# RWKV head-pair scan on one Trainium2 core: another order of the per-round work on TensorE, VectorE and ScalarE

## What is computed

```python
def update(s, w_t, k_t, v_t, kk_t, a_t):
    sa = einsum('ebhvk,ebhk->ebhv', s, kk_t)
    return s * w_t[..., None, :] - sa[..., :, None] * (kk_t * a_t)[..., None, :] \
           + v_t[..., :, None] * k_t[..., None, :]
# per token: s = update(s, ...); y = einsum('ebhvk,ebhk->ebhv', s, r)
# w, a: low-rank products of the input; kk: normalised keys
# out: ((group_norm(y) * ln_w + ln_b + bonus) * g) @ w_o
# bonus = (sum over a head of r * k_dir * r_k) * v;  g = sigmoid(x @ g1) @ g2
```

## Time and profile before

| | |
|---|---|
| median of 3 runs | 2686.97 us |
| the profiled execution | 2688.55 us, span 2686.8 us |
| busy in the span | PE 87%, PE weight loads 72%, DVE 35%, ACT 25%, POOL 32% |
| mean granted TensorE clock | 0.929 |
| first w16 of the scan to the last z | 1636.08 to 2201.91 us |

### The profile page before, as it was taken

How to read it: one execution, slowest core, us unless ns; L and a number is a source line. 1 busy time by engine, 2 the same in 40 slices (tenths; PEclk the granted TensorE clock), 3 DMA queues, 4 the chain that set the end, 5 groups by cost and what they waited for, 6 DMA issues and landing times. The chain is left out here.

```text
span 2686.8 us, 50294 instructions
## 1 busy us (share of the span) xinstructions
PE 2336.4 (87%) x22240; PEld 1946.8 (72%) x22240; DVE 944.5 (35%) x1475; ACT 662.8 (25%) x1032; POOL 854.6 (32%) x699
## 2 busy tenths in 40 slices
PE   5999877989699999999499957888888868999997
PEld 3778754555499999999169946777677755788786
DVE  3100175980500000222782035656565641200123
ACT  4110165421400000121321123433343312211111
POOL 2233200001144444343054413222332305466562
PEclk8999988989799999999599968999999978999998
DMA  5555600001021212111123421111111112232231
GB/s 215 215 204 210 221 33 16 1 32 47 17 70 62 62 62 62 63 63 48 18 85 111 134 59 33 39 36 37 39 39 37 22 64 63 78 94 94 86 97 68
DMA packets 139266, 204.06 MB, mean 76 GB/s; under 512 B 87783, under 2 KB 97511, under 8 KB 131912
## 3 DMA queue, kind: packets, MB, share of 16 engines
q1 hardware_dynamic: 139080, 201.26, 23.8%
HBM read 183.93 MB, written 17.30 MB: 75 GB/s over the span
## 5 line engine op out<-in xcount | busy, mean ns | idle before, releaser
L258 POOL CAST TMP_r<-WR 128x1024 fp32r<-128x1024 f32 x120 | 126.1, 1051 | 751.3 <-DMA WR<-in_ffn_w_dram 438.0
L277 PE MATMUL PS<-H_r,TMP_r 128*128 128x384 f32 (+1 forms) x1088 | 330.2, 359 | 15.4 <-DVE Y_r L492 15.4
L277 PE MATMUL PS<-Y_r,TMP_r 128*128 128x384 f32 (+1 forms) x1088 | 329.8, 358 | 3.7 <-DVE H_r L492 3.7
L260 POOL TENSOR_TENSOR WR_r<-WR,TMP_r 128x1024 fp32r<-128x1024 f32 x120 | 289.1, 2409 | 9.6
L415 DVE TENSOR_TENSOR P<-TMP,PS 128x768 f32 (+1 forms) x44 | 36.1, 821 | 562.4 <-PE PS L277 562.4
L277 PEld LDWEIGHTS PS<-H_r,TMP_r 128*128 128x128 f32 x1088 | 202.0, 190 | 33.0 <-DVE Y_r L492 17.3
L277 PEld LDWEIGHTS PS<-Y_r,TMP_r 128*128 128x128 f32 x1088 | 201.3, 189 | 19.3 <-DVE H_r L492 4.0
L277 PE MATMUL PS<-H_r,WR_r 128*128 128x384 f32 x736 | 191.6, 342 | 0.0
L268 POOL CAST TMP_r<-WR 128x1024 fp32r<-128x1024 f32 x68 | 84.3, 1240 | 322.0 <-DMA WR<-in_rw_w_rkv_dram 167.2
L270 POOL TENSOR_TENSOR WR_r<-WR,TMP_r 128x1024 fp32r<-128x1024 f32 x68 | 165.8, 2439 | 5.5
L398 ACT ACTIVATE TMP<-PS 128x768 f32<-128x768 f32 (+1 forms) x44 | 31.0, 705 | 525.9 <-PE PS L277 525.9
(11 more groups left out here) (307 smaller groups left out, 4480.5 us busy)
## 6 DMA issues: line engine op xcount, KB each, us to landing
WR<-in_ffn_w_dram SPq DMA_DIRECT2D x88, 512.0 KB, 3.5
TMP<-in_mod_w_dram SPq DMA_DIRECT2D x40, 1024.0 KB, 4.9
WR<-in_down_dram SPq DMA_DIRECT2D x44, 512.0 KB, 3.5
WR<-in_mix_w_in_dram SPq DMA_DIRECT2D x24, 512.0 KB, 7.0
WR<-in_rw_w_rkv_dram SPq DMA_DIRECT2D x24, 512.0 KB, 4.2
P<-in_mod_w_dram SPq DMA_DIRECT2D x4, 2048.0 KB, 21.7
vkr_dram<-extra SPq DMA_DIRECT2D x16, 384.0 KB, 4.8
scan_front<-vkr_dram SPq DMA_DIRECT2D x16, 384.0 KB, 3.1
```

Of the source, the lines that this page charges most:

```text
L258: nc.gpsimd.tensor_copy(hi, raw).then_inc(weights_hi, 1)
L260: nc.gpsimd.tensor_tensor(lo, raw, hi.bitcast(F32), ALU.subtract).then_inc(weights_split, 1)
L277: last = nc.tensor.matmul(PS[:, bank + b, 0:h1 - h0], w, x[:, h0:h1], start=k + p == 0, stop=k == CT - 1 and p == 2)
```

## The change

The same instructions are issued with the same operands, but in another order within a round, and two rounds' border is crossed by one of them:

- `lora(c, 0)` and its two Tanh evictions are issued at the end of the round for pair c (on PE between `kr` and `var`), instead of `lora(n, 0)` at the start of the next.
- PE: `oo_0` before A_0, `y32_1` before both; `cg` moves from between `mr_1` and `mr_2` to between `n_0` and `yt`, and DVE's `bonus` product behind `n_0`; kT_0, kT_1 and tV move in front of the chain.
- Between the chain's steps stand first the four transposes tB and tK, then KD_0, CK_0, KD_1, CK_1 and `kk`; before, it was the four products first, and then the transposes. BV_0 stands before `ys`, BV_1 between `ys` and `mean`.
- DVE: the mask of w16_0 stands before the first cumulative sum `scan_0` (L2583); `accr` comes after step 2 instead of step 4; the masks of KD and CK after steps 6 to 9 instead of 2 to 6.
- ACT: the evictions follow; `kc` and `ksq` of pair c now stand before tK_0 and tK_1 of pair n.
- SP and POOL keep their order.

The core of the diff (the tables `PEM`, `DV`, `AC`, `FRONT` repeat the loops' order):

```diff
                 if here(n):
-                    lora(n, 0)
...
                     transition(i, 0)
                     transition(i, 1)
+                if here(n):
+                    turned(n, 0)
+                if here(i):
+                    transition_rest(i)
+                    states(i, 0)
                     b = front("cg", i)
...
-                    transition_rest(i)
-                    states(i, 0)
                     pe.wait_ge(dve_done, DV["mL_1", i])
                     outputs_inside(i)
+                if here(n):
+                    turned(n, 1)
+                if here(i):
                     states(i, 1)
+                if here(n):
+                    pe.wait_ge(v_in, 16 * n + 16)
+                    tokens(n, "tV", VD[n % 2])
+                if here(i):
                     pe.wait_ge(dve_done, DV["n_1", i])
                     chain(i, 1)
...
                 if here(i):
-                    pe.wait_ge(act_done, AC["sq", i])
-                    PEM.done(turned_sums(3, FIN, 4), "var", i)
+                    outputs_carried(i)
+                if here(n):
+                    value_gram(n, 1)
+                if here(i):
+                    pe.wait_ge(act_done, AC["ys", i])
+                    PEM.done(nc.tensor.matmul(PS[:, 3, 0:L], HONES, YS, start=True, stop=True), "mean", i)
...
                     PEM.done(last, "kr", c)
-                if here(n):
-                    value_gram(n, 1)
-                if here(i):
+                    lora(c, 0)
+                if here(i):
+                    pe.wait_ge(act_done, AC["sq", i])
+                    PEM.done(turned_sums(3, FIN, 4), "var", i)
...
             for i, n, c in ROUNDS:
+                if here(i):
+                    level(i, 0, 0)
                 if here(n):
                     sums(n, 0)
                 if here(i):
-                    level(i, 0, 0)
                     level(i, 0, 1)
```

More of the change, by code:

```diff
@@ L1953, in hybrid_dit_kernel @@
         PEM = Marks(pe_done, (
[7 rows of a table removed]
-        DV = Marks(dve_done, (
[6 rows of a table removed]
-            (2, "kmax krec"), (0, "rec"), (2, "kmul"), (0, "f1 f2 z")))
[7 rows of a table added]
+        DV = Marks(dve_done, (
[6 rows of a table added]
+            (2, "kmax krec"), (0, "cen"), (2, "kmul"), (0, "rec f1 f2 z")))
         AC = Marks(act_done, (
[3 rows of a table removed]
[3 rows of a table added]
         PO = Marks(pool_done, ((1, "s00 s10 s01 s11 zero sub turn"),))
-        FRONT = ("l00 l10 l01 l11 A_0 A_1 cg KD_0 CK_0 KD_1 CK_1 tV tB_0 tK_0 tB_1 tK_1 kT_0 kT_1 kk BV_0 kr BV_1").split()
+        FRONT = ("l00 l10 l01 l11 A_0 A_1 cg kT_0 kT_1 tV tB_0 tB_1 tK_0 tK_1 KD_0 CK_0 KD_1 CK_1 kk BV_0 BV_1 kr").split()
         FRONT_TURN = {at: k for k, at in enumerate([at for at in PEM if at[0] in FRONT])}
@@ L2337, in scan_pe @@
                 if here(i):
[L2338 to L2343, removed]
+                    pe.wait_ge(dve_done, DV["y32_1", i])
+                    solve(i, "oo_1", [(1, j) for j in range(4)])
                 if here(n):
@@ L2387, in scan_pe @@
                 if here(i):
-                    chain(i, 6)
+                    pe.wait_ge(dve_done, DV["n_1", i])
+                    chain(i, 1)
                 if here(n):
@@ L2391, in scan_pe @@
                 if here(i):
+                    chain(i, 2)
+                if here(n):
+                    tokens(n, "tB_1", AA[1])
+                if here(i):
+                    chain(i, 3)
+                if here(n):
+                    pe.wait_ge(dve_done, DV["kt_0", n])
+                    tokens(n, "tK_0", SU[0])
+                if here(i):
+                    chain(i, 4)
+                if here(n):
+                    pe.wait_ge(dve_done, DV["kt_1", n])
+                    tokens(n, "tK_1", SU[1])
+                if here(i):
+                    chain(i, 5)
+                if here(n):
+                    gram_keys(n, 0)
+                if here(i):
+                    chain(i, 6)
+                if here(n):
+                    gram_rest(n, 0)
+                if here(i):
                     chain(i, 7)
                 if here(n):
-                    tokens(n, "tK_0", SU[0])
+                    gram_keys(n, 1)
                 if here(i):
@@ L2397, in scan_pe @@
                 if here(n):
-                    tokens(n, "tB_1", AA[1])
+                    gram_rest(n, 1)
                 if here(i):
                     chain(i, 9)
[L2401 to L2404, removed]
-                if here(n):
-                    turned(n, 0)
-                if here(i):
-                    outputs_carried(i)
-                if here(n):
-                    turned(n, 1)
-                if here(i):
-                    pe.wait_ge(act_done, AC["ys", i])
-                    PEM.done(nc.tensor.matmul(PS[:, 3, 0:L], HONES, YS, start=True, stop=True), "mean", i)
                 if here(c):
@@ L2417, in scan_pe @@
                     PEM.done(turned_sums(b, KS, 6), "kk", c)
+                if here(i):
+                    chain(i, 10)
                 if here(n):
@@ L2551, in scan_act @@
                                                  paired(front_bank("BV_1", n)), ACT.Copy), "bv_1", n)
+                if here(i):
+                    act.wait_ge(dve_done, DV["cen", i])
+                    AC.done(nc.scalar.activation(FIN, YS, ACT.Square), "sq", i)
+                    act.wait_ge(pe_done, PEM["var", i])
+                    AC.done(nc.scalar.activation(VROOT, PS[:, 3, 0:8], ACT.Sqrt, scale=1.0 / CH, bias=small[:, 3:4]),
+                            "groot", i)
+                    act.wait_ge(dve_done, DV["rec", i])
+                    AC.done(nc.scalar.activation(FIN.rearrange("p (k t) -> p k t", t=TC),
+                                                 VROOT.unsqueeze(2).broadcast_to([128, 8, TC]), ACT.Copy), "vwide", i)
+                if here(c):
+                    for e in range(2):
+                        tangent(c, e, 0)
         def scan_dve(v):
@@ L2711, in scan_dve @@
                     states(i, 0)
+                    v.wait_ge(pe_done, PEM["cg", i])
+                    DV.done(nc.vector.tensor_tensor(EB, PS[:, front_bank("cg", i), 0:L], VD[i % 2][:, 0:L], ALU.mult),
+                            "bonus", i)
                 if here(n):
@@ L2726, in scan_dve @@
                 if here(n):
+                    after("acc_1", n)
+                    DV.done(nc.vector.tensor_tensor(acc, acc, RDIR, ALU.mult), "accr", n)
+                if here(i):
+                    steps(i, 3, 4, 5, 6)
+                if here(n):
                     mask_keys(n, 0)
                 if here(i):
-                    steps(i, 3)
+                    steps(i, 7)
                 if here(n):
@@ L2732, in scan_dve @@
                 if here(i):
-                    steps(i, 4)
-                if here(n):
-                    after("acc_1", n)
-                    DV.done(nc.vector.tensor_tensor(acc, acc, RDIR, ALU.mult), "accr", n)
-                if here(i):
-                    steps(i, 5)
+                    steps(i, 8)
                 if here(n):
@@ L2745, in scan_dve @@
                 if here(i):
-                    steps(i, 7, 8, 9, 10)
-                    v.wait_ge(pe_done, PEM["mean", i])
-                    v.wait_ge(act_done, AC["ys", i])
-                    DV.done(nc.vector.scalar_tensor_tensor(YS, PS[:, 3, 0:L], -1.0 / CH, YS, ALU.mult, ALU.add), "cen", i)
+                    steps(i, 10)
                 if here(c):
```

80 lines of the change are left out of this document (29 added, 51 removed), and 32 rows, old and new, of tables (AC, DV, PEM).

## The result

| | before | after |
|---|---|---|
| median of 4 runs each | 2685.99 us (2681.32 to 2687.38) | 2659.06 us (2657.89 to 2661.46) |
| ratio | | 0.9902, 95% interval 0.9887 to 0.9918 |
| the profiled execution | 2688.55 us | 2657.89 us, span 2656.1 us |

The change makes the kernel faster by 27 us, 1.0%. The forecast was 2673: the sign is right and the time lies just inside the range, but the gain is twice the one forecast (13.5).

A forecast was written before the change was run, and what follows sets the result against it. No engine is full; a path between engines, with TensorE's waits, bounds the round. 39.35 + 17.3 + 12.25 + 3.0 = 71.9 us against 73.69; with rounds 0, 6 and 7, -13.5 in all: 2673 us, range 2658 to 2692.

The forecast's parts named there:

- w16 to the chain: Part 1, first inversion product to first chain step: 39.35 us, with issue gaps of 1.05 instead of 2.73.
- Steps 1 to 5 at 1.18: Start of the chain: with one transpose each, these steps take 1.18 us each.
- KD_0 at 9.0 us after step 1: In the chain: KD_0 starts at 9.0 us instead of 5.1, its bank's eviction queued behind kc and ksq.
- the keys' wait: In the chain, kc waits for loaded keys and delays KD_0: chain 17.3 us instead of 15.42; without it 13.4.
- a loss of 3.0 a round: Time lost to TensorE's low granted clock in each full round: 3.0 us, set between 1.2 and 3.8.
- Part 3 is 12.25: From the end of step 10 to the next w16: 12.25 us instead of 16.17, clock loss counted separately.
- Round 0's +1.9: Round 0: scan_0, which ran while w16 waited for data, now comes behind the w16_0 mask: +1.9 us.
- Round 6's 1.5 for the clock: Low-clock loss in round 6, which has no pair c: 1.5 us within its 63.8, against 67.07 before.
- Round 7's -1.4: Round 7 only has cg moved, which saves 1.4 us of issue gap.
- B: Rival, chance 0.15: the issue gaps stay; round 73.6 us, total 2687, no change.
- C: Rival, chance 0.18: slower by the keys' wait, keys landing 5.8 us after issue plus low clock; 75.9 a round, 2697.
- D: Rival, chance 0.15: faster, clock stays high (loss 1.0) and gaps shrink to 0.5; 69.35 a round, 2656 us.

The follow-up runs named there:

- the idle run: Fastest version (keys' instructions behind tK evictions, lora behind var) plus a TensorE wait ahead of KD_0 for pair c's ksq: 2642.32 us, ratio 0.9849.
- the run with the keys late: Kernel after, with ScalarE's kc and ksq of pair c moved behind the evictions of tK_0 and tK_1: 2627.7 us, ratio 0.9784.
- the fastest version: Kernel after, with kc and ksq behind the tK_0 and tK_1 evictions and lora between var and vr on TensorE: 2616.95 us, ratio 0.974.

## Why the prediction was right and wrong

**Right.** The walk held at nearly every place. w16 to the chain: 39.35 forecast, 39.12 measured, but here two errors cancel, which is luck: the gaps are 0.3 instead of 1.05, and the part without them is 38.8 instead of 38.3. Steps 1 to 5 at 1.18: 1954.90 to 1956.08. The keys' landing 3.3 us after issue. KD_0 at 9.0 us after step 1: 8.96. Without the keys' wait 13.4: 13.2 to 13.6. The gaps close and the keys' wait opens, both as forecast. lora about 1 us idle behind kmul: 1.09.

**Wrong by size: the clock.** The step that failed is "I take a loss of 3.0 a round", with "nearer the upper end because of that idle piece". By the windows the low clock cost some 1.65 us a round in after: 1.24 in the chain (18.54 less the estimated 17.3) and 0.41 behind it (11.86 less 11.45). The kernel before lost 2.8: 2.1 in the chain (17.56 less 15.42), 0.7 behind it (14.71 less 14.01). So the forecast kept the loss as large as it had been, and it fell by more than a third. These windows of the kernel before are its chains in rounds 2, 3 and 4 and its last parts in rounds 3 and 4:

```profile
1823.96:1842.09 18.13, 14.04 (x274) 11.99 (x275) 10.27 (x30) 5.55 (x7) 9.01 (x20) 0.81 0.36 95
1897.99:1916.97 18.98, 15.66 (x274) 13.54 (x275) 10.23 (x30) 5.55 (x7) 7.79 (x17) 0.73 0.38 93
1971.69:1987.11 15.42, 10.92 (x270) 9.37 (x270) 10.22 (x30) 4.71 (x7) 8.88 (x20) 1.00 0.34 104
1916.97:1930.98 14.01, 12.46 (x210) 10.29 (x208) 4.00 (x8) 8.85 (x15) 0.00 (x0) 1.00 0.16 16
1987.11:2003.28 16.17, 14.47 (x213) 12.10 (x213) 4.01 (x8) 9.59 (x16) 0.00 (x0) 0.89 0.24 24
```

and these, of after, its chains in rounds 3, 4 and 6 and its last parts in rounds 3 and 4:

```profile
1884.00:1903.56 19.56, 14.39 (x296) 13.11 (x298) 10.20 (x31) 6.85 (x9) 10.09 (x22) 0.83 0.39 92
1954.90:1973.12 18.22, 13.82 (x296) 12.33 (x298) 10.09 (x31) 6.85 (x9) 8.41 (x18) 0.91 0.46 104
2093.18:2105.75 12.57, 11.14 (x302) 9.82 (x304) 10.05 (x30) 3.85 (x5) 8.05 (x18) 1.00 0.12 34
1903.56:1915.01 11.45, 9.10 (x174) 7.30 (x171) 2.12 (x5) 5.10 (x8) 0.00 (x0) 1.00 0.16 16
1973.12:1984.68 11.56, 9.21 (x174) 7.29 (x170) 2.11 (x5) 5.21 (x8) 0.00 (x0) 0.99 0.06 6
```

Five of before's six chains ran partly low, two of them at 0.73 and 0.74; the one I built the walk on, round 4, was the only clean one. In after all six do, four at 0.91 and two at 0.82 and 0.83. So the idle piece does bring the low clock each time, as feared, but less of it. A mean clock of 0.91 over 18.22 us is 3.3 us at half speed. Worked out so for every chain it is 4.5 us a round in after and 6.1 in before. It is also somewhat cheaper by the microsecond: behind KD_0 VectorE's masks pace the chain and a slower TensorE partly hides behind them, while before the low clock fell on steps that TensorE paced. By the idle run 0.95 us for 3.5 low ones; in before 3.6 for 10.2. That reading of the price is argued from the rows, not tested by itself. The bounds of the term, 1.2 and 3.8, were misread too: by these windows round 4 lost 2.16 (16.17 less 14.01) and round 3 lost 3.56 (18.98 less 15.42), and the rest of what made round 3 longer was its gaps, 3.7 us against 2.7.

**Wrong by size: the last part.** "Part 3 is 12.25": it is 11.45 where the clock is high. I had taken the clock's share of round 4's last part as 1.2; the clean one of round 3 shows 2.16, so the part without it was shorter on both sides.

**Smaller terms.** The first part makes 0.2. Together -1.35 (clock), -0.8 (last part), -0.2: the 2.4 by which a round came out under 71.9, 14.3 us over six, of which the clock is 8.1. Round 0's +1.9 did not come. Round 6's 1.5 for the clock did not either (12.57 at 1.00 above), and its sum is 1.8 lower. Round 7's -1.4 failed the other way: 56.52 against 56.61, though its gaps fell from 2.52 to 1.25; what took that back I did not find. 14.3 + 1.9 + 1.8 - 1.3 is 16.7, which but for rounding is the difference between the 30.3 that the windows show and the 13.5 forecast.

**The rivals.** B falls: the gaps went from 3.3 to 0.3. C's mechanism was there, but its price was not: the keys landed in 3.3 us. D gave 69.35 a round and 2656 us, the nearest numbers, and it is half right: the gaps did shrink below 0.5, while the clock did not stay high. Its point lies below the range, 2658 to 2692, that was said to take in most of it, and the measured 2659 only just within. C's 74.2 a round is where the kernel would be as fast as before; slower by 0.2% would need 75.1. What I should have seen is that a loss of 2.8 a round stood in before already, behind waits that the new order mostly takes away: the new loss had to be worked out for the new waits, not set near the old one. With the clock at 1.2 I would have had about 2662, but that bound rested on a misreading.

**What the total hides.** Over the six rounds the change won 13.8 us in the first part, about half of it by the place of `cg`, 17.1 in the last, in good part because work left it, and 25.6 in the chain (17.56 to the 13.29 of the run with the keys late; about half of that is the low clock of before's chains), and gave 31.5 back at KD_0. The total, -25, shows nothing of that.

## What to carry to other kernels

In an engine that works strictly in order, an eviction behind a wait for a DMA holds a PSUM bank, and through it another engine: put what waits for a load behind the evictions whose banks the neighbour needs next. Put slow work of few instructions (here three wide products) ahead of long runs of tiny matmuls, and fill the time in which another engine makes an operand with work that is ready (lora behind var, not ahead of it). When a part shrinks, see whether waiting or work has left it. Cut before and after into parts at the same events, take the instance at full clock as the part's length, and price the low clock on both sides in the same way.

## What the runs showed of the hardware

- In the long runs of 64x64 fp32 matmuls of this kernel something passes 256 instructions in 3.5 to 4.0 us: 96 matmuls and 96 weight loads more cost 2.6 us a round where TensorE needs 1.4. The Trainium skill ("Runtime: NRT & Kernel Launch", instruction fetch mechanics) calls crossing a block mostly hidden; if the gaps are such crossings, as the count of 256 suggests, here it is not.
- The granted clock fell at nearly every idle piece of 3 to 5 us ahead of KD_0: in all six chains of after and in five of six with the idle piece put in. The twelve chains of the two versions without it stayed at 0.98 to 1.00. One of six with the piece stayed at 1.00; what decided that the traces do not say. Such a piece is not the only thing the clock falls behind: five of before's six chains ran partly low behind waits of at most 2.1 us, and in the fastest version the last part ran low in three of six rounds with no idle piece over 0.73 us in the chain ahead of it.
- A wait's named releaser can be the wrong one of two that end close together: `sq` is named, `kmul` ended 0.25 us later.
